# Storing the high and low halves of a weight piece float by float in one tile

## The chip, the cores and the metric

The kernel runs on one core of a Trainium2 chip. A core has the engines TensorE (PE in the profile; PEld is its weight load, which overlaps the matmuls), VectorE (DVE), ScalarE (ACT), GpSimd (POOL) and SyncE (SP), and 16 DMA engines that move data between HBM and the on-chip memory SBUF. The metric is the device time of one execution in microseconds (us), less is better.

## The reference, cut to what matters

Two layers over 256 tokens of width 1024, everything in float32. Each layer has three token mixers behind one input projection, then a channel mixer: a dense SwiGLU in layer 0, and top-2-of-8 expert SwiGLU in layer 1.

```python
for l in range(DEPTH):                       # DEPTH = 2
    h = rms_norm(x, g_mix[l])
    u = jnp.einsum('bsd,dc->bsc', h, w_in[l])          # pool, conv, q, k, v, forget, gates
    y_pool, y_conv, y_attn = ...                       # from slices of u
    gates = jax.nn.sigmoid(u[..., OFF_G:] + b_gate[l]).reshape(B, S, N_BRANCH, D)
    merged = (gates[:, :, 0] * (y_pool @ w_br_pool[l]) + gates[:, :, 1] * (y_conv @ w_br_conv[l])
              + gates[:, :, 2] * (y_attn @ w_br_attn[l]))
    x = x + jnp.einsum('bsd,de->bse', merged, w_out[l])
    h = rms_norm(x, g_ffn[l])
    x = x + (swiglu(h, ffn_w1[0], ffn_w3[0], ffn_w2[0]) if l % 2 == 0
             else moe_ffn(h, router_w[0], exp_w1[0], exp_w3[0], exp_w2[0]))
```

## The kernel before, in words

**Weights in pieces.** All weights come as 427 pieces of 1 MB: 128 partitions by 2048 floats. SP loads them in order into six buffers `raw` (line 250). Each piece is then split in two, so that a product of float32 numbers can be made of matmuls in the format `float32r`. ACT copies the piece, rounding it, into `w_high` (`split_high`, line 256). DVE subtracts `w_high` from `raw` and writes the rest to `w_low` (`split_low`, line 260). There are three buffers of each half (`SPLIT = 3`), so ACT may begin piece c when PE has finished piece c-3 (the semaphore `used`). The six tiles are each [128, 2048], and every instruction reads and writes them without gaps.

**Products.** `products` (lines 267 to 273) makes three matmuls of each term: high by high (L270), high by low (L271), low by high (L272). Each matmul loads its own stationary operand of 128 columns (a LDWEIGHTS record) and streams a moving operand past it. In the profile's names the moving operand stands first: `bank<-h_high,w_high` streams `h_high` past weights from `w_high`.

**Which side the weights are on.** Pieces come in a fixed order, which is written out by hand for every engine.
- Mixers (29 pieces a layer, `MIX_PIECES`): the weights are stationary and 256 tokens stream past (`channel_unit`, line 1026), except in three pieces a layer (V, V and pool, lines 1113 to 1121), where 128 tokens are stationary and 256 columns of the weights stream.
- Dense stage (33 pieces, `dense`): the weights are stationary, 256 columns of activations stream.
- Expert stage (336 pieces, `experts`, from piece number `MOE0`): the gathered tokens are stationary and 512 columns of the weights stream.

A piece in the mixers or the dense stage is 16 terms, so 48 matmuls of 256 columns. A piece in the expert stage is 8 terms, so 24 matmuls of 512 columns.

Of the kernel before, what the change touches and what calls it, by code (L numbers as in the profile page):

```python
# [22 lines left out]
F32 = mybir.dt.float32  # L23
F32R = mybir.dt.float32r
# [3 lines left out]
ACT = mybir.ActivationFunctionType  # L28
AX_X = mybir.AxisListType.X

P = 128
# [19 lines left out]
RAW = 6  # L51
SPLIT = 3
PIECE = 2048
# [23 lines left out]
MOE0 = BASE[1] + MIX_PIECES  # L77
# [35 lines left out]
def trunk(nc, xt, consts, params, w_in, w_br_pool, w_br_conv, w_br_attn, w_out,  # L113
          ffn_w1, ffn_w3, ffn_w2, exp_w1, exp_w3, exp_w2, out):
    with ExitStack() as ctx:
        def sb(name, shape, dt=F32):
            return ctx.enter_context(nc.sbuf_tensor(name, shape, dt))

        def sem(name):
            return ctx.enter_context(nc.semaphore(name))  # L120
# [2 lines left out]


        raw = [sb(f"raw{i}", [P, PIECE]) for i in range(RAW)]
        wh = [sb(f"w_high{i}", [P, PIECE], F32R) for i in range(SPLIT)]
        wl = [sb(f"w_low{i}", [P, PIECE], F32R) for i in range(SPLIT)]

        xT = sb("xT", [P, KC, S])
        hf = sb("h_full", [P, KC, S])  # L130
# [80 lines left out]
        s = {n: sem(n) for n in names}  # L211
# [11 lines left out]
        def fold(ap, k):  # L223
            return ap.rearrange("p (k n) -> p k n", k=k)


        def num(c, r):
            return c if isinstance(r, int) and r == 0 else r * RAW + c
# [18 lines left out]
        def load_piece(sp, c, r, src, k):  # L247
            if not (isinstance(r, int) and c < RAW):
                sp.wait_ge(s["split_done"], num(c - RAW + 1, r))
            sp.dma_start(fold(raw[c % RAW][:], k), src).then_inc(raw_in[c % RAW], 16)  # L250

        def split_high(act, c, r=0):
            act.wait_ge(raw_in[c % RAW], 16 * (c // RAW + 1) if isinstance(r, int) else r * 16 + 16 * (c // RAW + 1))
            if not (isinstance(r, int) and c < SPLIT):
                act.wait_ge(s["used"], num(c - SPLIT + 1, r))
            nc.scalar.activation(wh[c % SPLIT][:], raw[c % RAW][:], ACT.Copy).then_inc(s["high_done"], 1)  # L256

        def split_low(dve, c, r=0):
            dve.wait_ge(s["high_done"], num(c + 1, r))
            nc.vector.tensor_tensor(wl[c % SPLIT][:], raw[c % RAW][:], wh[c % SPLIT][:].bitcast(F32),  # L260
                                    ALU.subtract).then_inc(s["split_done"], 1)

        def take_piece(pe, c, r=0, k=KC):
            pe.wait_ge(s["split_done"], num(c + 1, r))
            return fold(wh[c % SPLIT][:], k), fold(wl[c % SPLIT][:], k)

        def products(pe, dst, terms, start=True, stop=True):

# [83 lines left out]
        def _(act):  # L352
# [7 lines left out]
            def norm(nn, ahead=()):  # L360

                act.wait_ge(s["norm_stats"], nn + 1)
                nc.scalar.activation(rt[:, 0:S], bank[3][:, 0:S], ACT.Sqrt, bias=A(0, A_EPS),
                                     scale=1.0 / D).then_inc(s["norm_root"], 1)
                for c in ahead[:1]:
                    split_high(act, c)
                for g in range(4):
                    act.wait_ge(s["norm_h"], 8 * nn + 2 * g + 2)
                    nc.scalar.activation(hH[:, 2 * g:2 * g + 2, :], hf[:, 2 * g:2 * g + 2, :],
                                         ACT.Copy).then_inc(s["h_high_done"], 1)  # L370
                for c in ahead[1:]:
                    split_high(act, c)

            def mixer(l):
                b = BASE[l]
                norm(2 * l, [0, 1] if l == 0 else [])
                split_high(act, b + 2)
                if l == 0:
                    act.wait_ge(s["const_in"], 16)
# [214 lines left out]
        def _(dve):  # L594
# [29 lines left out]
            def mixer(l):  # L624
                b = BASE[l]
                norm(2 * l)
                if l == 0:
                    split_low(dve, 0)
                    dve.wait_ge(s["f_raw"], l + 1)
                    nc.vector.tensor_copy(f8, bank[3][0:8, S:2 * S]).then_inc(s["f_copied"], 1)  # L630
                    split_low(dve, 1)
                split_low(dve, b + 2)
                step(nc.vector.memset(zp[:, :, 0:PAD], 0.0))

# [358 lines left out]
        def _(pe):  # L993
# [48 lines left out]
            def mixer(l):  # L1042
# [67 lines left out]

                for n in range(P_BRPOOL):
                    H, L = take_piece(pe, b + n)
                    if n in (P_V, P_V + 1, P_POOL):
                        bank_free(l, n)
# [31 lines left out]
                for n in range(P_BRPOOL, P_OUT):  # L1146
                    first, K, units = {P_BRPOOL: (0, 2, 4), P_BRCONV: (2, 2, 4), P_BRATTN: (4, 4, 2), P_BRATTN + 1: (4, 4, 2)}[n]
                    need = {P_BRPOOL: LOW_ORDER[0], P_BRCONV: LOW_ORDER[2], P_BRATTN: 6, P_BRATTN + 1: 6}[n]
                    pe.wait_ge(s["y_low_done"], 6 * l + need)
                    H, L = take_piece(pe, b + n, 0, K)  # L1150
                    for m in range(units):
                        channel_unit(l, u, H, L, yH[:, first:first + K, :], yL[:, first:first + K, :], 256 * m)
                        u += 1
                for n in range(P_OUT, MIX_PIECES):
                    def part_ready(k):
                        if k % 2 == 0:
                            pe.wait_ge(s["merged_low"], 4 * l + k // 2 + 1)

                    H, L = take_piece(pe, b + n)
                    channel_unit(l, u, H, L, hH, hL, 0, before=part_ready if n == P_OUT else None)  # L1160
                    u += 1
                    if n > P_OUT:
                        norm_stats(2 * l + 1, n - P_OUT - 1)
# [234 lines left out]
```

## Time and profile before

| | before |
|---|---|
| median of two runs | 1715.64 us (1713.95 to 1717.34) |
| profiled execution | 1714.5 us |
| its span, first to last instruction | 1712.4 us |
| TensorE's mean granted clock | 0.99 of 2.4 GHz |
| PE busy | 1662.2 us, 97% |
| DVE busy | 1283.0 us, 75% |
| ACT busy | 1053.5 us, 62% |

The span is the time of one execution taken by the profiler. A busy share is an average over stages that differ: roughly, layer 0's mixer ends at 240 us, the dense stage at 440 us, layer 1's mixer at 670 us, and the expert stage fills the rest. Matmuls are pipelined and their ends are modelled, so the distance between the starts of neighbouring matmuls says more than a matmul's duration.

### The profile page before, as it was taken

What the parts mean: (1) busy time and instruction counts of PE and PEld (TensorE: products, weight loads), DVE (VectorE), ACT (ScalarE), POOL (GpSimd) and SP (SyncE); (2) the same over time, 40 slices, a digit from 0 to 9 for tenths busy, and PEclk for the clock granted to TensorE, in tenths of its full rate; (3) what the DMA queues carried; (4) which work ended last, traced back from release to release, by engine and by line L of the source; (5) the groups of instructions that cost most, each with busy time, mean ns of one, the idle gap of its engine ahead of it and who ended that gap; (6) DMA issues with size and microseconds to landing.
All of it is one profiled execution on the core that took longest, in us unless ns stands there. A gap on an engine that the chain in (4) does not pass through costs nothing.

```text
span 1712.4 us, 25143 instructions
## 1 busy us (share of the span) xinstructions
PE 1662.2 (97%) x9630; PEld 1444.0 (84%) x9630; DVE 1283.0 (75%) x1078; ACT 1053.5 (62%) x902; POOL 51.9 (3%) x52
## 2 busy tenths in 40 slices
PE   7999989999899998999999999999999999999998
PEld 7988889999798888788788788788788788788787
DVE  5964854454697485888887888888888888888886
ACT  5544444453544445677677677677677677677675
POOL 0131000000013100000000000000000000000000
PEclk9999999999999999999999999999999999999999
DMA  9543445555354342699899899899899899899894
GB/s 336 167 133 100 147 136 174 185 179 185 120 156 144 99 148 85 241 381 370 294 375 364 304 377 348 320 374 337 335 373 337 332 375 337 325 381 339 322 381 155
DMA packets 231292, 452.46 MB, mean 264 GB/s; under 512 B 6992, under 2 KB 80720, under 8 KB 231120
## 3 DMA queue, kind: packets, MB, share of 16 engines
q1 hardware_dynamic: 231248, 451.82, 74.2%
q8 instruction: 34, 0.56, 0.1%
q14 instruction: 10, 0.08, 0.0%
HBM read 450.74 MB, written 1.05 MB: 264 GB/s over the span
## 4 chain that ended last, share of the span: by engine, by line
PE 89%; DVE 8%; issue 2%; ACT 1%; DVEq 0%; DMA 0%; ACTq 0%
PE bank L270 27%; PE bank L271 26%; PE bank L272 26%; DVE w_low L260 3%; PE bank L1238 2%; PE bank L1254 1%; DVE xacc L930 1%; PE bank L998 1%; DVE h_full L691 1%; PE bank L1088 1%; DVE gate L686 1%; ACT w_high L256 1%; DVE h_full L617 1%; PE bank L1107 0%; DVE rinv L607 0%
## 5 line engine op out<-in xcount | busy, mean ns | idle before, releaser
L260 DVE TENSOR_TENSOR w_low<-raw,w_high 128x2048 fp32r<-128x2048 f32 x427 | 975.5, 2290 | 300.6 <-ACT w_high L256 300.0
L256 ACT ACTIVATE w_high<-raw 128x2048 fp32r<-128x2048 f32 x427 | 818.3, 1917 | 418.6 <-PE bank L272 416.0
L270 PE MATMUL bank<-w_high,hg_high 128*128 128x512 f32 x896 | 354.9, 396 | 8.8 <-DVE w_low L260 8.8
L272 PE MATMUL bank<-w_high,hg_low 128*128 128x512 f32 x896 | 349.8, 390 | 0.0
L271 PE MATMUL bank<-w_low,hg_high 128*128 128x512 f32 x896 | 349.8, 390 | 0.0
L270 PE MATMUL bank<-h_high,w_high 128*128 128x256 f32 x1056 | 304.0, 288 | 9.2 <-DVE h_low L612 4.8
L271 PE MATMUL bank<-h_low,w_high 128*128 128x256 f32 x1056 | 298.8, 283 | 0.0
L272 PE MATMUL bank<-h_high,w_low 128*128 128x256 f32 x1056 | 298.2, 282 | 0.0
L270 PEld LDWEIGHTS bank<-h_high,w_high 128*128 128x128 f32 x1056 | 200.5, 190 | 14.6 <-issue 9.4
L270 PEld LDWEIGHTS bank<-w_high,hg_high 128*128 128x128 f32 x896 | 168.8, 188 | 45.3 <-DVE w_low L260 11.0
L271 PEld LDWEIGHTS bank<-h_low,w_high 128*128 128x128 f32 x1056 | 200.4, 190 | 1.6 <-issue 1.4
L272 PEld LDWEIGHTS bank<-h_high,w_low 128*128 128x128 f32 x1056 | 200.1, 189 | 0.0
L272 PEld LDWEIGHTS bank<-w_high,hg_low 128*128 128x128 f32 x896 | 168.7, 188 | 36.3
L271 PEld LDWEIGHTS bank<-w_low,hg_high 128*128 128x128 f32 x896 | 168.8, 188 | 33.7
L270 PE MATMUL bank<-w_high,g_high 128*128 128x512 f32 x448 | 175.1, 391 | 0.0
L272 PE MATMUL bank<-w_high,g_low 128*128 128x512 f32 x448 | 174.4, 389 | 0.0
L271 PE MATMUL bank<-w_low,g_high 128*128 128x512 f32 x448 | 174.3, 389 | 0.0
L272 PEld LDWEIGHTS bank<-w_high,g_low 128*128 128x128 f32 x448 | 84.1, 188 | 17.6
L271 PEld LDWEIGHTS bank<-w_low,g_high 128*128 128x128 f32 x448 | 84.1, 188 | 17.2
L270 PEld LDWEIGHTS bank<-w_high,g_high 128*128 128x128 f32 x448 | 84.1, 188 | 17.1
L347 POOL TENSOR_SCALAR decay<-cst,fg 128x128 f32<-128x128 f32 x48 | 51.7, 1092 | 518.8 <-DVE fg L792 409.4
L945 DVE TENSOR_TENSOR gu<-sl,bank 128x512 f32<-128x512 f32 x56 | 38.2, 682 | 31.5 <-PE bank L272 31.5
(225 smaller groups left out, 1580.8 us busy)
## 6 DMA issues: line engine op xcount, KB each, us to landing
raw<-exp_w SPq DMA_DIRECT2D x336, 1024.0 KB, 5.7
raw<-w_in SPq DMA_DIRECT2D x42, 1024.0 KB, 5.2
raw<-ffn_w SPq DMA_DIRECT2D x33, 1024.0 KB, 5.3
raw<-w_out SPq DMA_DIRECT2D x8, 1024.0 KB, 5.3
raw<-w_br_attn SPq DMA_DIRECT2D x4, 1024.0 KB, 5.0
raw<-w_br_pool SPq DMA_DIRECT2D x2, 1024.0 KB, 5.2
raw<-w_br_conv SPq DMA_DIRECT2D x2, 1024.0 KB, 5.4
cst<-consts SPq DMA_DIRECT2D x1, 1280.0 KB, 13.8
```

What stands on the lines that cost most here:

```text
L256: nc.scalar.activation(wh[c % SPLIT][:], raw[c % RAW][:], ACT.Copy).then_inc(s["high_done"], 1)
L260: nc.vector.tensor_tensor(wl[c % SPLIT][:], raw[c % RAW][:], wh[c % SPLIT][:].bitcast(F32), ALU.subtract).then_inc(s["split_done"], 1)
L270: pe.matmul(dst, lh, rh, start=start and i == 0, stop=False)
L271: pe.matmul(dst, lh, rl, start=False, stop=False)
L272: last = pe.matmul(dst, ll, rh, start=False, stop=stop and i == len(terms) - 1)
L347: nc.gpsimd.tensor_scalar(decay[:, h % 2, k, :], C(m), lf[:, tile, h:h + 1], None, ALU.mult).then_inc(s["decays"], 1)
L617: nc.vector.scalar_tensor_tensor(out=hf[:, k, :], in0=xT[:, k, :], scalar=A(nn // 2, (A_GMIX, A_GFFN)[nn % 2] + k), in1=rinv[:, 0:S], op0= ...
L686: ins = nc.vector.scalar_tensor_tensor(out=to, in0=g, scalar=1.0, in1=fold(bank[UNIT_BANK[u]][:], 2), op0=ALU.add, op1=ALU.mult)
L691: ins = nc.vector.tensor_tensor(dst, dst, g, ALU.add)
L930: nc.vector.tensor_tensor(dst, dst, bank[b][:], ALU.add).then_inc(s["m_add"], 1)
L945: nc.vector.tensor_tensor(gu[:], sl[:], bank[1][:], ALU.mult).then_inc(s["m_mult"], 1)
L1238: ins = pe.matmul(bank[GATHER_BANKS[g]][:, k * P:k * P + P], src[:, t, ch * P:ch * P + P], perm[:, t, :], start=t == 0, stop=t == TT - 1)
```

## The change

The six tiles `w_high0..2` and `w_low0..2` become three tiles `w_halves0..2` of [128, 4096]. In the mixers and the dense stage (pieces before `MOE0`) the halves are views with a step of two floats: float 0 of the high half, float 0 of the low half, float 1 of the high half, and so on. In the expert stage the first 2048 floats are the high half and the next 2048 the low half, each without gaps. The space is the same. Every engine issues the same instructions in the same order with the same waits; only tile names and access patterns differ.

```diff
-        wh = [sb(f"w_high{i}", [P, PIECE], F32R) for i in range(SPLIT)]
-        wl = [sb(f"w_low{i}", [P, PIECE], F32R) for i in range(SPLIT)]
+        whl = [sb(f"w_halves{i}", [P, 2 * PIECE], F32R) for i in range(SPLIT)]
...
+        def halves(c):
+
+            order = "p (two n) -> p two n" if c >= MOE0 else "p (n two) -> p two n"
+            both = whl[c % SPLIT][:].rearrange(order, two=2)
+            return both[:, 0], both[:, 1]
+
...
-            nc.scalar.activation(wh[c % SPLIT][:], raw[c % RAW][:], ACT.Copy).then_inc(s["high_done"], 1)
+            nc.scalar.activation(halves(c)[0], raw[c % RAW][:], ACT.Copy).then_inc(s["high_done"], 1)
...
-            nc.vector.tensor_tensor(wl[c % SPLIT][:], raw[c % RAW][:], wh[c % SPLIT][:].bitcast(F32),
+            high, low = halves(c)
+            nc.vector.tensor_tensor(low, raw[c % RAW][:], high.bitcast(F32),
                                     ALU.subtract).then_inc(s["split_done"], 1)
...
-            return fold(wh[c % SPLIT][:], k), fold(wl[c % SPLIT][:], k)
+            return tuple(fold(half_, k) for half_ in halves(c))
```

## Rows read from the trace of the kernel before

**Rows 1.** The page: busy tenths in 40 equal slices, clock, DMA share.

```profile
PE   7999989999899998999999999999999999999998
DVE  5964854454697485888887888888888888888886
ACT  5544444453544445677677677677677677677675
PEclk9999999999999999999999999999999999999999
DMA  9543445555354342699899899899899899899894
```

**Rows 2.** The page: the chain that ended last, share by engine.

```profile
PE 89%; DVE 8%; issue 2%; ACT 1%; DVEq 0%; DMA 0%; ACTq 0%
```

**Rows 3.** Windows: each engine's busy us (instructions), clock, DMA share, GB/s.

```profile
20.00:100.00 80.00, 79.45 (x632) 75.30 (x631) 68.56 (x82) 40.63 (x41) 8.52 (x9) 1.00 0.70 220
180.00:210.00 30.00, 26.57 (x217) 25.49 (x216) 25.22 (x30) 12.54 (x14) 0.00 (x0) 1.00 0.52 166
250.00:427.00 177.00, 177.00 (x1483) 176.82 (x1482) 82.73 (x51) 79.62 (x59) 0.00 (x0) 1.00 0.58 184
```

**Rows 4.** The page: groups of instructions by line, xcount, busy us, mean ns.

```profile
L260 DVE TENSOR_TENSOR w_low<-raw,w_high 128x2048 fp32r<-128x2048 f32 x427 | 975.5, 2290 | 300.6 <-ACT w_high L256 300.0
L256 ACT ACTIVATE w_high<-raw 128x2048 fp32r<-128x2048 f32 x427 | 818.3, 1917 | 418.6 <-PE bank L272 416.0
L270 PE MATMUL bank<-h_high,w_high 128*128 128x256 f32 x1056 | 304.0, 288 | 9.2 <-DVE h_low L612 4.8
L270 PEld LDWEIGHTS bank<-h_high,w_high 128*128 128x128 f32 x1056 | 200.5, 190 | 14.6 <-issue 9.4
```

**Rows 5.** Groups by line and shape: the other matmuls on the weights before the experts.

```profile
L270 PE MATMUL bank<-g_high,w_high 128*128 128x256 f32 x176 | 49.9, 283 | 2.9 <-DVE g_low L816 2.9
L270 PE MATMUL bank<-y_high,w_high 128*128 128x256 f32 x128 | 36.4, 285 | 3.0 <-DVE gate L686 2.3 <-DVE h_full L686 0.7
L270 PE MATMUL bank<-w_high,h_high 128*128 128x256 f32 x96 | 27.8, 289 | 0.0
```

**Rows 6.** Timeline, expert stage, PE: start us, us, engine, line, instruction.

```profile
1002.25 0.39 PE L270 MATMUL bank<-w_high,hg_high 128*128 128x512 f32 x1
...
1003.38 0.39 PE L272 MATMUL bank<-w_high,hg_low 128*128 128x512 f32 x1
```

**Rows 7.** Timeline, end of an expert job, PE: the gathers of 128 columns.

```profile
807.60 1.98 PE L1238 MATMUL bank<-perm,ht_high 128*128 128x128 f32 x16
809.42 1.95 PE L1238 MATMUL bank<-perm,ht_low 128*128 128x128 f32 x16
811.21 0.41 PE L1310 MATMUL bank<-cst,perm_gated 128*128 128x128 f32 x2
```

**Rows 8.** Timeline, start of the kernel, PE and PEld, where the granted clock was 0.50.

```profile
15.99 0.41 PE L272 MATMUL bank<-h_high,wf_low 128*128 128x256 f32 x1
15.99 0.33 PEld L270 LDWEIGHTS bank<-h_high,wf_high 128*128 128x128 f32 x1
16.20 0.41 PE L270 MATMUL bank<-h_high,wf_high 128*128 128x256 f32 x1
```

**Rows 9.** The chain that ended last in time, end of a mixer: start us, us, what.

```profile
180.46 1.93 ACT w_high L256
182.41 2.29 DVE w_low L260
...
197.71 2.29 DVE w_low L260
...
202.65 2.20 DVE w_low L260
```

**Rows 10.** Groups by line, DVE alone, from 20 to 100 us.

```profile
L260 DVE TENSOR_TENSOR w_low<-raw,w_high 128x2048 fp32r<-128x2048 f32 x14 | 31.9, 2286 | 8.1 <-ACT w_high L256 8.1
```

## The prediction

> **What bounds the kernel now.** I read the slices first [rows 1]: PE is at 9 tenths or more nearly everywhere, the clock is full, and DVE, ACT and DMA have room before the experts. The chain that ended last says the same: 89% of it is PE and 8% DVE [rows 2]. Then the windows [rows 3]. In the dense stage (250 to 427 us) PE is busy for all of 177 us while DVE works 82.7 us and ACT 79.6 us. So there a slower matmul costs its whole excess and a slower split costs nothing. At the end of a mixer (180 to 210 us) it is the other way: DVE is busy 25.2 of 30 us, and the chain runs through the splits [rows 9]. Between 20 and 100 us both are loaded: PE 79.5 and DVE 68.6 of 80 us.
>
> The change issues nothing new and removes nothing, and no instruction changes place. All that can move is how long an instruction takes that now touches every second float. In the expert stage the halves still lie without gaps, so its 1000 us stay, up to small effects of other addresses.
>
> **The price of a pair.** The dense window holds 1483 matmuls in 177 us [rows 3]: 0.119 us from one matmul of 256 columns to the next, each with its own load of 128 stationary columns. In the expert stage five steps take 1.13 us [rows 6]: 0.226 us for 512 columns. So the stream sets the pace, and 256 more columns cost 0.107 us. Gathers of 128 columns come every 0.113 us (32 of them in 3.61 us, [rows 7]), hardly less than those of 256. There the stream is short, so a load of 128 columns fits in 0.113 us at most. It is therefore hidden in a pair of 0.119, but with only 0.006 us to spare. It also follows the clock: at half clock a load's record is 0.33 us and the step 0.21 us [rows 8], against 0.19 us at full clock [rows 4].
>
> **What each reader and writer would have to cover.** No row of before has an access with a gap, so I compare spans of addresses. A strided operand covers twice the bytes that it uses.
> - *Stream of moving columns.* Now 512 floats, 2048 bytes a partition, in 0.226 us: 9.1 bytes a nanosecond. A strided stream of 256 columns covers 2048 bytes too. To stay at 0.119 us it would need 17 bytes a nanosecond, which no engine shows here. If the span counts, it takes what 512 columns take, 0.226 us.
> - *Load of stationary columns.* 128 floats, 512 bytes in 0.113 us. Strided, it covers 1024 bytes; in the same time that is 9.1 bytes a nanosecond, just what the stream shows that TensorE can be fed.
> - *DVE and ACT.* 8192 bytes in 2.290 and 1.917 us [rows 4]. Strided, 16384 bytes: 7.2 and 8.5 bytes a nanosecond, below 9.1.
>
> So I take it that span counts, and that 9.1 bytes a nanosecond is what can be had. Then only the moving stream gets slower.
>
> **The sum.** Weights stream in three pieces a mixer: 96 terms, so 288 matmuls [rows 5]. Each goes from 0.119 to 0.226 us: 288 x 0.107 = 30.8 us. Lower bound: 0, if a gap costs nothing. Upper bound: the same 30.8 us, since a doubled span is read as though all of it were used. I take the upper end, because it is nearest to the row of 512 columns. PE is full in this stretch and carries the cost to the end; ACT and DVE only gain room.
>
> Stationary loads on the weights: 1056 + 176 + 128 = 1360 terms [rows 4, 5], 4080 loads. I take 0 for them. The bounds are far apart: 0, or a load that doubles to 0.226 us and becomes the pace, 4080 x 0.107 = 437 us. The cover is the stream of the matmul before, and it has 0.006 us left. Beyond that each nanosecond costs 4.1 us, so 0 is the value by the bytes, not a safe one.
>
> Splits: 0, hidden behind PE in the dense stage. If they slow down, the end of each mixer pays (below).
>
> The profiled execution took 1714.5 us (span 1712.4 and 2.1 around it). 1714.5 + 30.8 = 1745.3; the median of the two runs is 1.1 us higher, so I say 1746.5.
>
> **A rule against it.** By the rows, a stream of 2048 bytes in 0.119 us has no precedent. The Trainium skill, "SBUF — State Buffer", in the note on SBUF cachelines under "Door 1: The DMA port swizzle", speaks of lines of 16 bytes, of which two hits are enough for full bandwidth. A step of two floats makes two hits in each line, so by that rule nothing at all slows down and the sum would be 0. That is the first rival. A second page is stricter for DVE: the "Vector Engine (DVE) Microarchitecture Reference", "Measured stream behaviour on trn2", wants runs of two adjacent words, and gives 1.73 ns per column for one source that hops at every element against 1.05 without hops. It does not measure a step of two. By it a split on DVE would be an estimated 3.7 us or so, which speaks for the third rival in part.
>
> **The rivals.**
> 1. *A step of two floats is free for everybody.* For it: TensorE is fed contiguously at 9.1 bytes a nanosecond, but nothing shows that this is the limit of its port. Against it: doubled spans are unprecedented. Time: 1715.6. Chance 0.30.
> 2. *The stationary load slows, and PE's pace with it.* For it: the cover of 0.006 us, and that a load takes about as long for 128 columns as a stream of 256, as if it read its operand twice. If it does so in two passes, each at the stream's rate, the strided load is as unprecedented as the strided stream. Against it: the bytes used per load are half of a stream's. Fully doubled: 1714.5 + 437 + 31 = 2182 us. A part is possible as well: at 25 ns too long for the cover it is 1714.5 + 102 + 31 = 1848. It decides when a load takes over 0.119 us. Chance 0.20 (0.15 near the full price, 0.05 in part).
> 3. *ACT and DVE slow, as far as double.* 14 splits stand between 20 and 100 us [rows 10]: 14 x 2.29 = 32 us more work, where DVE has 11.4 us free, so 21 us too much, 41 us for two mixers. On the chain at the mixers' ends and the dense stage's end stand 11 splits on DVE, as those of [rows 9], and 5 on ACT: 11 x 2.25 + 5 x 1.92 = 34 us. Together 1714.5 + 75 = 1790 us. For it: DVE reads one and writes one strided stream at once. Against it: 7.2 bytes a nanosecond is less than PE gets. Chance 0.06.
> 4. *It gets faster.* The pace of 0.119 is 0.012 above what 256 columns add (0.107). If part of this is the load and the stream colliding in memory and the new addresses part them, the gain ends where loads become the pace: 4368 matmuls x 0.006 = 26 us, or 52 us if the load is really as short as 0.107. That is 1663 to 1689 us. Nothing shows such collisions. Chance 0.04.
> 5. *My forecast:* only the moving stream slows. 1746.5 us, chance 0.40, with its own range of 1738 to 1765 (loads up to 4 ns over the cover).
>
> **How the numbers follow.** The point is the likeliest case. The range starts at 1710, below rival 1, and leaves out rival 4 (0.04). Above, it takes in rival 3 and the partial form of rival 2, so 1850, and leaves out the doubled load (0.15). 2% of the median is 34 us, about what can be told from no change here; slower means over 1750. My forecast lies 4 us below that line: three quarters of its chance fall within (0.30), one quarter beyond (0.10). Within 2%: 0.30 + 0.30 = 0.60. Slower: 0.10 + 0.20 + 0.06 = 0.36. Faster: 0.04.
>
> **What would show it.** In the profile of the changed kernel:
> - The steps between the matmuls that stream `w_halves` past `h_high` (V and pool pieces, around 60 to 80 us) are near 0.226 us. If they are 0.119, rival 1 holds.
> - In the dense stage the step stays at 0.119 us and the stage as long as now. If it is longer, rival 2 holds, and the LDWEIGHTS mean leaves 190 ns.
> - L260 and L256 keep their means of 2290 and 1917 ns in the first 670 us, give or take a few per cent. If not, rival 3 holds.
> - The expert stage from 720 us on is equally long, within 2 us.
> The prediction is wrong as a whole if TensorE's loads are read at the stream's full rate in two passes, since the cover there is thin.

## The result, and the profile after

The changed kernel takes 1751.36 us (median of two runs, 1750.40 to 1752.32) against 1715.64, a ratio of 1.021 with a 95% interval of 1.019 to 1.024. Its span is 1750.2 us against 1712.4, so 37.8 us more. The forecast was 1746.5.

The page of the changed kernel, first the busy us by engine, then PE's busy tenths in 40 slices and the clock:

```profile
PE 1699.7 (97%) x9630; PEld 1475.8 (84%) x9630; DVE 1284.4 (73%) x1078; ACT 1069.1 (61%) x902; POOL 48.0 (3%) x52
...
PE   7999989999899999899999999999999999999998
...
PEclk9999999999899999899999999999999999999999
```

PE is the bound as before [rows 1, 2], with 37.5 us more busy time; DVE works as long as before. The tenths of the granted clock show two slices of 8 that were 9 before.

The timeline of the changed kernel, PE alone, first the beginning of the three streamed pieces of layer 0's mixer, then their end:

```profile
60.26 0.39 PE L276 MATMUL bank<-w_halves,h_high 128*128 128x256 f32 x1
60.47 0.41 PE L277 MATMUL bank<-w_halves,h_high 128*128 128x256 f32 x1
...
93.47 0.42 PE L277 MATMUL bank<-w_halves,h_high 128*128 128x256 f32 x1
93.70 0.42 PE L278 MATMUL bank<-w_halves,h_low 128*128 128x256 f32 x1
```

The step is about 0.23 us, and the three pieces last 33.44 us from the first start to the last. In the kernel before the same two starts are these:

```profile
58.40 0.28 PE L270 MATMUL bank<-w_high,h_high 128*128 128x256 f32 x1
...
76.11 0.28 PE L272 MATMUL bank<-w_high,h_low 128*128 128x256 f32 x1
```

That is 17.71 us, so 15.73 us more in this mixer. Layer 1's mixer gives 15.72. Together 31.45 of the 37.8 us.

The groups of the changed kernel that answer to [rows 4], the splits by line and the loads of the stationary weights:

```profile
L266 DVE TENSOR_TENSOR w_halves<-raw,w_halves 128x2048 fp32r<-128x2048 f32 x427 | 975.8, 2291 | 337.8 <-ACT w_halves L261 337.1
L261 ACT ACTIVATE w_halves<-raw 128x2048 fp32r<-128x2048 f32 x427 | 835.0, 1956 | 444.6 <-PE bank L278 441.3
...
L276 PEld LDWEIGHTS bank<-h_high,w_halves 128*128 128x128 f32 x1056 | 208.7, 198 | 14.0 <-issue 9.0
```

DVE's mean stands at 2291 ns. ACT's mean is over all 427 pieces and hides that most are unchanged: in the first 715 us alone, where the halves are mixed, the group reads

```profile
L261 ACT ACTIVATE w_halves<-raw 128x2048 fp32r<-128x2048 f32 x93 | 193.9, 2087 | 181.8 <-PE bank L278 178.9 <-DMA raw<-w_in 2.6
```

that is 2087 ns against 1911 in the same stretch before. A load's record goes from 190 to 198 ns.

The table gives the length of each stage, from the starts of the same matmuls in the timelines of five kernels (E1 to E3 are explained below). A stage runs from the first matmul of one kind to the first of the next; only the rows of the streamed pieces and of the branches end with the start of their own last matmul, and the row of the dense stage too.

| stage, us | before | changed | E1 stream | E2 load | E3 apart |
|---|---|---|---|---|---|
| start to first piece | 21.1 | 22.6 | 21.0 | 20.9 | 21.5 |
| mixer 0: to the streamed pieces | 37.29 | 37.70 | 37.24 | 37.65 | 37.26 |
| the three streamed pieces | 17.71 | 33.44 | 33.58 | 17.72 | 17.71 |
| gates and heads | 104.98 | 105.90 | 105.15 | 105.80 | 104.98 |
| branches | 24.65 | 25.49 | 24.65 | 25.27 | 24.65 |
| output and norm | 36.16 | 34.85 | 34.64 | 36.42 | 34.70 |
| dense | 194.41 | 197.24 | 197.16 | 194.75 | 194.30 |
| mixer 1: streamed pieces alone | 17.71 | 33.43 | 33.57 | 17.73 | 17.71 |

The other parts of layer 1's mixer move much as those of layer 0's, up to the branches (0.42, 0.93 and 0.66 us more); its output part doesn't change. From the first gather to the end the changed kernel takes 1029.6 us, the kernel before 1029.5. So nothing of the loss lies in the expert stage.

### The profile page after: what moved, and what is told of

Same layout as the page of the kernel before. It is cut to its first block, busy times and chain, and to the rows that moved or that the text cites. A ratio compares the mean times of both kernels' runs of the same rounds, so it can differ in the third digit from the quotient of the medians.

```text
span 1750.2 us, 25143 instructions
## 1 busy us (share of the span) xinstructions
PE 1699.7 (97%) x9630; PEld 1475.8 (84%) x9630; DVE 1284.4 (73%) x1078; ACT 1069.1 (61%) x902; POOL 48.0 (3%) x52
## 4 chain that ended last, share of the span: by engine, by line
PE 89%; DVE 7%; issue 2%; ACT 1%; DMA 1%; DVEq 0%; SPq 0%; ACTq 0%
PE bank L276 27%; PE bank L278 27%; PE bank L277 27%; DVE w_halves L266 3%; PE bank L1244 2%; PE bank L1260 1%; DVE xacc L936 1%; ACT w_halves L261 1%; DMA raw<-w_in 1%; PE bank L1094 1%; PE bank L1004 1%; PE bank L1113 0%; PE bank L1096 0%; PE bank L1057 0%; PE bank L1095 0%
## 5 line engine op out<-in xcount | busy, mean ns | idle before, releaser
L266 DVE TENSOR_TENSOR w_halves<-raw,w_halves 128x2048 fp32r<-128x2048 f32 x427 | 975.8, 2291 | 337.8 <-ACT w_halves L261 337.1
L261 ACT ACTIVATE w_halves<-raw 128x2048 fp32r<-128x2048 f32 x427 | 835.0, 1956 | 444.6 <-PE bank L278 441.3
L276 PE MATMUL bank<-w_halves,hg_high 128*128 128x512 f32 x896 | 354.9, 396 | 8.8 <-DVE w_halves L266 8.8
L277 PE MATMUL bank<-w_halves,hg_high 128*128 128x512 f32 x896 | 349.7, 390 | 0.0
L278 PE MATMUL bank<-w_halves,hg_low 128*128 128x512 f32 x896 | 349.7, 390 | 0.0
L276 PE MATMUL bank<-h_high,w_halves 128*128 128x256 f32 x1056 | 306.3, 290 | 8.5 <-DVE h_low L618 4.8
L278 PE MATMUL bank<-h_high,w_halves 128*128 128x256 f32 x1056 | 299.7, 284 | 0.0
L277 PE MATMUL bank<-h_low,w_halves 128*128 128x256 f32 x1056 | 299.1, 283 | 0.0
L276 PEld LDWEIGHTS bank<-h_high,w_halves 128*128 128x128 f32 x1056 | 208.7, 198 | 14.0 <-issue 9.0
L277 PEld LDWEIGHTS bank<-h_low,w_halves 128*128 128x128 f32 x1056 | 208.1, 197 | 1.5 <-issue 1.4
L278 PEld LDWEIGHTS bank<-h_high,w_halves 128*128 128x128 f32 x1056 | 208.5, 197 | 0.0
L276 PEld LDWEIGHTS bank<-w_halves,hg_high 128*128 128x128 f32 x896 | 168.6, 188 | 45.3 <-DVE w_halves L266 11.0
L277 PEld LDWEIGHTS bank<-w_halves,hg_high 128*128 128x128 f32 x896 | 168.8, 188 | 33.7
L276 PE MATMUL bank<-w_halves,g_high 128*128 128x512 f32 x448 | 175.1, 391 | 0.0
L277 PE MATMUL bank<-w_halves,g_high 128*128 128x512 f32 x448 | 174.3, 389 | 0.0
```

Source lines behind the costliest of these rows:

```text
L261: nc.scalar.activation(halves(c)[0], raw[c % RAW][:], ACT.Copy).then_inc(s["high_done"], 1)
L266: nc.vector.tensor_tensor(low, raw[c % RAW][:], high.bitcast(F32), ALU.subtract).then_inc(s["split_done"], 1)
L276: pe.matmul(dst, lh, rh, start=start and i == 0, stop=False)
L277: pe.matmul(dst, lh, rl, start=False, stop=False)
L278: last = pe.matmul(dst, ll, rh, start=False, stop=stop and i == len(terms) - 1)
```

## The experiments

Two theories stood against each other after the result. **A**: the strided stream costs what 512 columns cost, and that is nearly everything. **B**: the loads and the splits carry a good part. E1 to E3 divide the change by who reads the strided weights. E4 to E7 ask what sets the price of a strided read: my argument had been the span of addresses, and the same numbers fit whole lines of 16 bytes.

**E1, only the streamed pieces float by float**

```diff
-            order = "p (two n) -> p two n" if c >= MOE0 else "p (n two) -> p two n"
+            order = "p (two n) -> p two n" if c - (BASE[1] if c >= BASE[1] else 0) not in (P_V, P_V + 1, P_POOL) else "p (n two) -> p two n"
```

> Only the three pieces a mixer whose weights stream past the tokens (V, V, pool) are stored float by float; all other pieces have their halves apart. Theory A (only the strided stream costs, and it costs what 512 columns cost): 288 matmuls go from 0.118 to 0.228 us, so 31 to 32 us more than before, ratio 1.018 to 1.019, and a load's record stays at 188 to 190 ns everywhere. Rival B (the loads and the splits carry a good part of the 36 us): 15 to 25 us more, ratio 1.009 to 1.015.

Measured: 1748.56 us (five runs, 1748.04 to 1750.04) against 1714.52, ratio 1.0202 (1.0188 to 1.0216), so 34 us. The streamed pieces take 15.87 and 15.86 us more, 31.7 together, as theory A says; the total is 2 to 3 us over what was expected. The rest of about 2 us is a balance of parts in which no operand has a gap: the dense stage is 2.8 us longer, layer 0's output part 1.5 shorter, the stretch between the dense stage and the next mixer 0.8 shorter, and layer 1's output part 1.4 longer. Half of the dense stage's 2.8 us lie behind its last wait of PE. The windows of E1 around it:

```profile
442.00:446.00 4.00, 1.32 (x12) 1.12 (x10) 1.31 (x2) 1.89 (x3) 0.00 (x0) 1.00 0.00 0
446.00:450.00 4.00, 3.79 (x19) 3.82 (x20) 2.89 (x3) 3.98 (x3) 0.00 (x0) 0.57 0.00 0
```

After PE's idle time the granted clock (the last but two number) is 0.57 on average, mostly the lower level of 1.2 GHz, so PE makes 19 matmuls in 3.8 us. The changed kernel has the same:

```profile
446.00:450.00 4.00, 1.22 (x11) 1.01 (x9) 1.38 (x2) 2.00 (x3) 0.00 (x0) 0.97 0.00 0
450.00:454.00 4.00, 3.90 (x21) 3.93 (x22) 2.76 (x2) 3.98 (x3) 0.00 (x0) 0.60 0.00 0
```

and the kernel before, after the same wait, does not:

```profile
427.00:431.00 4.00, 1.11 (x9) 0.94 (x9) 1.38 (x2) 2.49 (x3) 0.00 (x0) 1.00 0.00 0
431.00:435.00 4.00, 4.00 (x36) 4.00 (x35) 3.43 (x2) 3.83 (x4) 0.00 (x0) 1.00 0.02 3
```

PE is idle for 2.9 us there in all of them. Behind it the last 96 matmuls of the stage take 14.5 us at full clock (before, E2, E3) and 15.9 at the lower one (changed, E1), so this is 1.4 us; the other 1.3 us are at the stage's beginning, where the clock is low in each of the kernels and stays so for longer beyond the first matmul in these two. Reaching the wait late doesn't decide it: E6 below takes the time of before, reaches the wait as early as the kernel before, and has the lower clock too:

```profile
426.00:430.00 4.00, 1.96 (x17) 1.76 (x15) 0.69 (x1) 1.25 (x3) 0.00 (x0) 1.00 0.00 0
430.00:434.00 4.00, 3.15 (x15) 3.18 (x16) 2.88 (x2) 3.98 (x3) 0.00 (x0) 0.58 0.00 0
```

Its dense stage takes 197.0 us, as the changed kernel's. So the dense stage's 2.8 us can't be put down to the gap, in E1 not at all and in the changed kernel but for 0.3 us (E2).

**E2, all but the streamed pieces float by float**

```diff
-            order = "p (two n) -> p two n" if c >= MOE0 else "p (n two) -> p two n"
+            order = "p (two n) -> p two n" if c >= MOE0 or c - (BASE[1] if c >= BASE[1] else 0) in (P_V, P_V + 1, P_POOL) else "p (n two) -> p two n"
```

> The counterpart: all pieces of the mixers and the dense stage are stored float by float, except the three a mixer whose weights stream. Theory A: the stream steps fall back to 0.118 us and what stays is the small rest, 3 to 6 us over before, ratio 1.002 to 1.004, with load records near 197 ns in place of 190 and ACT's splits near 2.05 us. Rival B: 10 to 20 us over before, ratio over 1.006.

Measured: 1719.83 us against 1714.52, ratio 1.0034 (1.0021 to 1.0048), so 5.3 us. The streamed pieces are back at 17.7 us. In its trace, loads take 198 ns and ACT's splits 2070 ns in the first 715 us. 3.6 us of the excess lie in the mixers: 0.36, 0.82 and 0.62 us in layer 0's first, gate and branch parts, about as much in layer 1. The dense stage has 0.3 more. The rest, 1.5 us in layer 1's output part, goes with a granted clock of 0.89 there (638.9 to 654 us), where the kernel before has 1.00 (635.1 to 648.7). B falls: loads and splits cost some 4 us, not 15. With E1 the two parts add up to 39.3 us, against 36.5 for the whole change by its ratio, which agrees within the intervals.

E2 also tells which of the two it is, mostly. The mean step between neighbouring matmuls whose loads are strided, short waits left out, in layer 0: in the gate and head part 118.2 ns before, 118.3 in E1, and 119.4 in E2 and in the changed kernel; in the branch part 117.8 before and in E1, 120.3 in E2, 121.7 in the changed kernel. With some 550 and 190 such steps that is 0.5 to 0.7 us in each part. So most of the excess lies in PE's own pace, where its loads are strided, and not in waits for the splits.

**E3, the new tile, nothing mixed**

```diff
-            order = "p (two n) -> p two n" if c >= MOE0 else "p (n two) -> p two n"
+            order = "p (two n) -> p two n" if True else "p (n two) -> p two n"
```

> The new tile of 4096 floats, but with the halves apart in every stage, so that only the addresses of the halves differ from before. Theory A: same time as before, ratio 0.998 to 1.002, every mean as before. Rival C (the new addresses collide otherwise in memory, and part of the loss is from that): 2 to 5 us over before.

Measured: 1715.08 us against 1714.52, ratio 1.0006 (0.9997 to 1.0015). Moving the halves in memory does nothing that can be seen; the cost is the gap.

**E4, strides alone**

A kernel that loads one tile of 4096 floats a partition, copies it to the float32r tiles `mov` and `sta`, and runs groups of the same matmul on lines of their own. Its core:

```python
def step(t, s, n, at=0):
    return t[:, at:at + n * s].rearrange("p (n s) -> p n s", s=s)[:, :, 0]
def runs(t, g, n):
    return t[:, 0:2 * n].rearrange("p (n two g) -> p two n g", two=2, g=g)[:, 0]
...
            for i in range(32):
                pe.matmul(b[:, 0:256], sta[:, 0:128], step(mov, 2, 256), **k)
```

> A kernel that computes nothing of the reference (it writes zeros): it runs matmuls, ACT copies and DVE subtractions alone, at several steps in floats, groups of 32 matmuls each. Theory A (a port of TensorE reads so many bytes of address span, or lines, a nanosecond): at full clock a stream of 256 columns takes 0.11 to 0.12 us at step 1, 0.22 to 0.23 at step 2, about 0.44 at step 4, or 0.43 flat from there if each column then costs a line of its own. In runs of two floats it costs as step 2, 0.22, since half of each line is skipped; in runs of four floats 0.22 if span counts and 0.11 if lines of 16 bytes count. At half clock step 2 costs as step 1, 0.213 us, since the pace is then 9.6 bytes a nanosecond. Rival D (TensorE fetches pairs of neighbouring floats, a granule of 8 bytes): runs of two cost nothing, 0.12, step 4 costs no more than step 2, and at half clock step 2 doubles to 0.43. Loads, streams of 128 columns: 0.11 us at step 1; at step 2 up to 0.115 if a load needs a new line every 1.7 ns, 0.22 if it read its operand in two passes at the stream's rate; at step 4 0.22. ACT writing at step 2: 2.05 to 2.1 us for 2048 floats against 1.9; DVE 2.2 us at step 2 and 3.5 us or more at step 4.

The timeline of E4, PE: each row is a group of 32 matmuls on one line. Streams of 256 columns at step 1, 2, 3, 4 and 8 (L132 to L140), in runs of two and of four (L142, L144), then the next group's start, that of contiguous columns once more:

```profile
51.85 4.00 PE L132 MATMUL bank<-mov,sta 128*128 128x256 f32 x32
55.69 7.42 PE L134 MATMUL bank<-mov,sta 128*128 128x256 f32 x32
62.93 7.43 PE L136 MATMUL bank<-mov,sta 128*128 128x256 f32 x32
70.18 7.64 PE L138 MATMUL bank<-mov,sta 128*128 128x256 f32 x32
77.65 7.15 PE L140 MATMUL bank<-mov,sta 128*128 128x256 f32 x32
84.62 7.54 PE L142 MATMUL bank<-mov,sta 128*128 128x256 f32 x32
91.97 3.95 PE L144 MATMUL bank<-mov,sta 128*128 128x256 f32 x32
95.76 3.99 PE L146 MATMUL bank<-mov,sta 128*128 128x256 f32 x32
```

The distance between two starts divided by 32 is the price of a matmul: 0.120, 0.226, 0.227, 0.233, 0.218 us for steps 1, 2, 3, 4, 8; 0.230 in runs of two; 0.118 in runs of four. So the span of addresses is not what counts: step 4 spans twice as much as step 2 and costs nearly the same, and runs of four with gaps span as much as step 2 and cost nothing. Neither theory on record holds as written: A had step 4 at 0.43 us or more, and D had runs of two for nothing. What holds of A is the line of 16 bytes.

The loads, first at step 2 and 4 under streams of 256 columns (L148, L150), then at steps 1 to 4 under streams of 128 columns, so that the load sets the pace (L152 to L158):

```profile
99.59 4.00 PE L148 MATMUL bank<-mov,sta 128*128 128x256 f32 x32
103.43 7.63 PE L150 MATMUL bank<-mov,sta 128*128 128x256 f32 x32
110.90 3.68 PE L152 MATMUL bank<-mov,sta 128*128 128x128 f32 x32
114.42 3.93 PE L154 MATMUL bank<-mov,sta 128*128 128x128 f32 x32
118.18 5.93 PE L156 MATMUL bank<-mov,sta 128*128 128x128 f32 x32
123.91 7.65 PE L158 MATMUL bank<-mov,sta 128*128 128x128 f32 x32
131.36 6.39 PE L160 MATMUL bank<-mov,sta 128*128 128x256 f32 x32
```

Under streams of 128 columns that is 0.110, 0.118, 0.179 and 0.233 us. The clock was not full in all of them: the last four matmuls at step 3 and the whole group at step 4 ran at a granted clock of 0.50. Up to there a load at step 3 took 0.174 us. Step 4 took 0.233 us at full clock too, under 256 columns. At steps 2, 3 and 4 a load touches 64, 96 and 128 lines of 16 bytes: 1.84, 1.81 and 1.82 ns for a line. Under a stream of 256 columns the load at step 2 is hidden here: 0.120 us with it and 0.120 without.

ACT and DVE in the same trace: ACT writes 2048 floats at step 1, 2 and 4 (L65, L69, L73); DVE reads its second operand at step 1 and 2 (L93, L97), reads and writes at step 2 (L101), reads at step 4 (L105):

```profile
137.78 5.79 ACT L65 ACTIVATE dst<-raw 128x2048 f32<-128x2048 f32 x3 [103.99 <-PE bank L160]
143.60 6.17 ACT L69 ACTIVATE dst<-raw 128x2048 f32<-128x2048 f32 x3
149.80 11.49 ACT L73 ACTIVATE dst<-raw 128x2048 f32<-128x2048 f32 x3
...
187.89 6.95 DVE L97 TENSOR_TENSOR rest<-raw,dst 128x2048 f32<-128x2048 f32 x3
194.87 6.95 DVE L101 TENSOR_TENSOR rest<-raw,dst 128x2048 f32<-128x2048 f32 x3
201.85 11.44 DVE L105 TENSOR_TENSOR rest<-raw,dst 128x2048 f32<-128x2048 f32 x3
```

A single instruction of these groups takes 1.91, 2.04 and 3.81 us on ACT; on DVE 2.29 at step 1 and 2, and 3.79 at step 4. At step 4, with a line for every float, that is 1.86 ns a line for ACT and 1.85 for DVE. At step 2 DVE has 2.24 ns for a line by its own pace and notices nothing. ACT has 1.87 ns for a line at step 2, which should just do by this price; it needs 1.99, and that stays unexplained.

**E5, how a stream can reach a line in 0.9 ns**

One thing does not fit a single reader: at step 4 a stream takes 256 lines in 0.233 us, 0.91 ns for each, half of what a load, ACT and DVE need. Theory E: two readers take the even and the odd columns in turn. Theory F: a stream is fast only in whole runs of four. The pattern that parts them reads two places 2048 floats apart in turn (`h`):

```python
def turns(t, s, n):
    return t[:].rearrange("p (h n) -> p n h", h=2)[:, 0:n // 2 * s].rearrange("p (n s) h -> p n s h", s=s)[:, :, 0]
```

> A kernel that computes nothing of the reference (it writes zeros): more streams and loads alone, 32 matmuls a group. In the first strides kernel a stream of 256 columns took 0.120 us at step 1, 0.226 at step 2, 0.227 at 3, 0.233 at 4, 0.218 at 8, 0.230 in runs of two with gaps and 0.118 in runs of four; loads took 0.110, 0.118, 0.179 and 0.233 us at steps 1 to 4. Theory E (two readers take the even and the odd columns of a stream in turn, and each needs 1.8 ns for a new line of 16 bytes, a load has one such reader): columns taken in turn from two distant places cost 0.12 us when each place is read at step 1, 0.12 at step 2 too (two hits a line for each reader), and 0.23 at step 4. Theory F (a stream is at full rate only in whole runs of four neighbouring floats, and at half rate otherwise): 0.22 to 0.23 us for all three of them. Starts one or two floats off a line: 0.12 in both. Loads at step 8 and 16 cost 0.23 us as at step 4, since no load needs more than one line a column. Streams of 512 columns: 0.227 and 0.44 us. At half clock, bursts of ten after an idle time: step 1 0.213, step 2 0.213 to 0.24 (E and F), and a load at step 4 0.233 us, the same in ns as at full clock, if the 1.8 ns is a time of the memory and not of TensorE's clock; 0.45 if it is of the clock.

The timeline of E5, PE: steps 1 and 2 for comparison (L98, L100), then two places in turn, each read at step 1, 2 and 4 (L102, L104, L106), then the next start:

```profile
91.35 4.00 PE L98 MATMUL bank<-mov,sta 128*128 128x256 f32 x32
95.19 7.42 PE L100 MATMUL bank<-mov,sta 128*128 128x256 f32 x32
102.43 3.75 PE L102 MATMUL bank<-mov,sta 128*128 128x256 f32 x32
106.02 4.00 PE L104 MATMUL bank<-mov,sta 128*128 128x256 f32 x32
109.86 7.42 PE L106 MATMUL bank<-mov,sta 128*128 128x256 f32 x32
117.10 4.12 PE L108 MATMUL bank<-mov,sta 128*128 128x256 f32 x32
```

0.112, 0.120 and 0.226 us for the three, against 0.226 for plain step 2. A stream that never has two neighbouring floats in a row runs at full speed, as long as every second column stays in its line for two hits. F falls, and E gives all ten prices of E4 and E5 with one number, to some 5%: a new line every 1.8 ns for each of two readers. That the hardware has two such readers is inferred from the prices.

Bursts of ten after an idle time, where the granted clock was 0.50, take 2.51 us at step 1, 2.62 at step 2 and 2.73 with the load at step 4. The steps inside them, from the third matmul on, are 0.213, 0.227 and 0.236 us. So at half clock a strided stream costs 0.014 us more and not 0.106, and takes the same 0.227 us as at full clock: the 1.8 ns is no time of TensorE's clock. Starts one and two floats off a line cost 0.124 and 0.117 us; loads at step 8 and 16 cost 0.240 and 0.223, as at step 4, at a granted clock of 0.62 and 0.50. The group of 512 contiguous columns fell into a stretch with a granted clock of 0.78 and is not used; at step 2 they took 0.453 us.

**E6, runs of four floats in place of single floats**

E1 with this in `halves` for the three streamed pieces (`RUN` is 4), and the raw piece viewed in the same groups for the splits:

```diff
+                both = whl[c % SPLIT][:].rearrange("p (n two g) -> p two n g", two=2, g=RUN)
```

> As the first experiment, only the three streamed pieces a mixer have their halves mixed, but in runs of four floats (16 bytes of the high half, 16 bytes of the low half) and not float by float. If whole lines are what counts (theory E or F), the streams' step is back at 0.118 us and the time is that of before, ratio 0.999 to 1.002. If the span of addresses counts (my reading in the prediction), the step stays at 0.226 and the time at 1.018 to 1.020.

Measured: 1715.16 us against 1714.57, ratio 1.0003 (0.9994 to 1.0012). The halves are still side by side and the span is doubled, but every line that is touched is used whole, and the 34 us of E1 are gone. The timeline of E6, PE, in a streamed piece:

```profile
70.51 0.28 PE L287 MATMUL bank<-w_halves,h_high 128*128 128x256 f32 x1
70.63 0.28 PE L288 MATMUL bank<-w_halves,h_high 128*128 128x256 f32 x1
```

The step is 0.12 us, where the changed kernel has 0.23.

**E7, float by float in the expert stage too**

```diff
-            order = "p (two n) -> p two n" if c >= MOE0 else "p (n two) -> p two n"
+            order = "p (two n) -> p two n" if False else "p (n two) -> p two n"
```

> Float by float in the expert stage too, where all 336 pieces are streamed: 4032 matmuls of 512 columns. From 0.227 to 0.44 us each: 4032 x 0.214 = 863 us more than the changed kernel, so about 2610 us (2590 to 2670). If the DMAs or the splits had been the pace there, less: under 2500.

Measured: 2643.19 us, one run. The step of a stream of 512 columns, from the timeline of E7:

```profile
1400.32 0.63 PE L276 MATMUL bank<-w_halves,hg_high 128*128 128x512 f32 x1
1400.77 0.63 PE L277 MATMUL bank<-w_halves,hg_high 128*128 128x512 f32 x1
```

0.450 us against 0.226 [rows 6]. 4032 x 0.223 = 899 us over 1751 is 2650, near the 2643 measured. The step was 0.01 us dearer than I had expected, as in E5 (0.453).

## Why the prediction was right, and where it was not

*The streams.* The term was 288 x 0.107 = 30.8 us; measured 31.45. The step went to 0.228, not 0.226. PE carried all of it, as said.

*Why they cost that.* Here the step "span counts, and 9.1 bytes a nanosecond is what can be had" was wrong, though its number came out. E4 shows the same price at step 4 with twice the span, and E6 shows a doubled span for nothing. What counts is how often a reader must open a new line of 16 bytes, 1.8 ns each. With a step of two the span and the lines grow by the same factor, so the row of 512 columns gave the right price for the wrong reason. That the largest term came out was luck in this: the same argument would have put step 4 at twice the price, and runs of four floats at that of step 2.

*The loads.* I took 0, warned of 0.006 us of cover, and gave 0.20 to a load that slows. By E4 a load at step 2 needs 0.118 us where a pair has 0.119. In the dense stage that was cover enough (0.3 us in all, E2). In the mixers it was not quite: there the steps were 117.8 to 118.2 ns, and grew by 1.2 ns in the gate and head part and by 2.5 to 3.9 in the branch part (E2's section). Why they went past the 0.118 us that a load takes alone (E4) is not shown. So a small form of my second rival came true, and my own sign for it, the load's record leaving 190 ns, showed it. Of the 4.2 us below about three quarters are this term that I had at 0. The rival's idea that a load reads its operand twice at the stream's rate falls: that would be over 0.22 us.

*The splits.* DVE stayed at 2290 ns as said. It came nowhere near the 3.7 us weighed under "A rule against it". ACT did not stay: 1911 to 2087 ns, more than "a few per cent", and more than the price of a line explains. It stands on the chain at the mixers' ends. The chain of the changed kernel there:

```profile
198.97 2.09 ACT w_halves L261
201.09 2.29 DVE w_halves L266
...
206.46 2.12 ACT w_halves L261
208.68 2.29 DVE w_halves L266
```

ACT's rows were 1.93 us before [rows 9]. Loads and splits together cost 4.2 us in the mixers (the table, the stages of both layers); E2 has 3.6. My sum had 0.

*What I left out.* The rest, 2.2 us in all, is no price of a gap, but for 0.3 us of the dense stage that E2 has too. The start came 1.5 us later, the dense stage was 2.8 us longer, and the output part of layer 0 and the stretch behind the dense stage were 2.1 us shorter together. Each of these parts has a stretch at the lower clock in some kernels or in all, and it lies elsewhere in each: the granted clock is 0.68 from 16 to 22 us before and 0.52 from 16 to 23 in the changed kernel; in layer 0's output part it is 0.89 before (205 to 221 us) and 1.00 in the changed kernel (225 to 239). Only one execution of each kernel is traced, and 15 of the kernel before alone range over 3.5 us, the shortest with the highest mean clock. So these 2.2 us may well fall out otherwise in the next execution. 31.45 + 4.2 + 2.8 + 1.5 - 2.1 = 37.85, the span's 37.8.

The profiled executions took 1714.5 and 1752.3 us, and the sum for the second was 1745.3. The 7.0 us between are 0.65 from the streams' step, 4.2 from loads and splits, and the 2.2 of the parts above. The median of the two runs, 1751.4, is 1.0 lower, and I had added 1.1 to the sum, hence 4.9 over the point.

*The chances.* The result fell at 1751.4, just over the line of 1750 that I had put a quarter of my own case behind. By the interval of 1.019 to 1.024 it can't be told from 2%, so which side of the line it fell on says nothing.

*The rules.* By the trace, a step of two floats doubles a stream. The rule of the Trainium skill in "SBUF — State Buffer" (note on SBUF cachelines) that two hits a line are enough holds by these runs for DVE (2.29 us at step 1 and 2), for a load nearly (0.110 to 0.118), for ACT with 7% off, and for the stream of a matmul at full clock not at all (0.120 to 0.226). At half clock it nearly does for the stream too (0.213 to 0.227).

## What to carry to other kernels

Put a price on a strided operand by counting new lines of 16 bytes a reader must open, at about 1.8 ns each, and compare with the pace at which the engine takes columns anyway. DVE takes a float32 step of two for nothing. A stationary load takes it for almost nothing under a stream of 256 columns (0.3 to 3.9 ns a matmul here), and the moving operand of a matmul at full clock pays nearly double. If two things must lie side by side, put them in runs of four floats, which cost nothing here, and keep a strided operand on the stationary side.

## What the runs showed of the hardware that I had not expected

- A stream takes alternate columns as if by two readers: 0.226 us at step 2, but 0.120 us when two distant places are read in turn, each at step 2.
- The price of a line is nearly the same for all that were measured: 1.81 to 1.86 ns for a load, for ACT writing and for DVE reading, with steps 3 and 4. Steps 8 and 16 give 1.70 (a stream, for each of its two readers) to 1.87 (a load).
- It doesn't follow TensorE's clock: at a granted clock of 0.50 the step of two costs 0.014 us a matmul in place of 0.106, and the load at step 4 takes 0.233 us at either level (E4).
- The same idle time of PE, 2.9 us, was followed by full clock in three traces (before, E2, E3) and by a mean of 0.57 to 0.60 in four (changed, E1, E6, E7), at 1.4 us a time. It is not the time at which the wait comes. What decides it stays open.
